# Norm roots and inverses on a fourth of the columns, and the first mixer's convolution dealt out anew

## What is computed

```python
def layer_norm(x, g, b):
    mu = jnp.mean(xf, axis=-1, keepdims=True)
    var = jnp.mean(jnp.square(xf - mu), axis=-1, keepdims=True)
    y = (xf - mu) * lax.rsqrt(var + EPS)
...
def conformer_conv(z, conv_w, conv_b, ln_g, ln_b):
    a, g = jnp.split(z, 2, axis=-1)
    h = a * jax.nn.sigmoid(g)
    h = causal_dwconv(h, conv_w, conv_b)      # 31 taps, 512 channels
    h = layer_norm(h, ln_g, ln_b)
    return jax.nn.silu(h)
...
# first layer ("even"): rms_norm, projection z, gelu on half of it,
#   layer norm "v", a spatial mixing, conformer_conv, output projection, FFN
# second layer ("odd"): attention, FFN; then rms_norm "final"
# second block, two layers: mixer, layer norm ln1, FFN, layer norm ln2
```

## Time and profile before

| | |
|---|---|
| median of 3 runs | 2508.51 us (2506.43 to 2509.03) |
| the profiled execution | 2508.29 us, its span 2506.6 us |
| TensorE matmuls busy | 96% of the span |
| VectorE, ScalarE, GpSimd busy | 56%, 43%, 5% |
| mean granted TensorE clock | 0.988 of full |

### The profile page before, as it was taken

One profiled execution on the slowest core, in us unless ns is written; L12 is line 12 of the kernel. 1 busy time (PEld: TensorE's weight loads), 2 busy tenths in 40 slices (PEclk: granted clock), 3 DMA queues, 4 the chain that ended last, 5 costly groups with the idle time before them and its releaser, 6 DMA issues.

```text
span 2506.6 us, 32833 instructions
## 1 busy us (share of the span) xinstructions
PE 2411.5 (96%) x11748; PEld 1912.8 (76%) x11748; DVE 1410.4 (56%) x2270; ACT 1083.7 (43%) x1673; POOL 125.7 (5%) x115
## 2 busy tenths in 40 slices
PE   8989999999999999999999989999989998999997
PEld 6657888887777888887777668888868766788885
DVE  5887777435765677732547764334353767533434
ACT  4444444326876444422447543233253663432322
POOL 0001000000000000001400010000113001000000
PEclk9999999999999999999999999999999999999999
DMA  4112222232121322222211122323222112232322
GB/s 174 61 42 93 99 94 99 94 101 68 59 67 59 101 92 100 92 101 96 103 60 35 51 72 96 100 94 101 93 100 74 43 35 76 76 101 93 101 93 76
DMA packets 57437, 210.61 MB, mean 84 GB/s; under 512 B 6478, under 2 KB 6880, under 8 KB 56960
## 3 DMA queue, kind: packets, MB, share of 16 engines
q1 hardware_dynamic: 56736, 204.51, 24.3%
q0 software_dynamic: 608, 4.81, 0.5%
HBM read 207.20 MB, written 2.10 MB: 83 GB/s over the span
## 4 chain that ended last, share of the span: by engine, by line
PE 67%; issue 22%; DVE 5%; POOLq 2%; ACT 2%; DVEq 1%; POOL 1%; DMA 0%; SPq 0%; ACTq 0%
PE PS L1150 12%; PE PS L1152 12%; PE PS L1151 12%; PE PS L1178 9%; PE PS L1180 9%; PE PS L1179 9%; PE PS L1209 1%; DVE CONV L1819 1%; DVE RSTD L1758 1%; POOLq L573 1%; PE PS L1264 1%; PE PS L1239 1%; PE PS L1242 1%; POOLq L582 1%; PE PS L1240 1%
## 5 line engine op out<-in xcount | busy, mean ns | idle before, releaser
L1744 DVE TENSOR_TENSOR WL<-RAW,WH 128x1024 fp32r<-128x1024 f32 x376 | 476.2, 1267 | 428.7 <-ACT WH L601 427.4
L1150 PE MATMUL PS<-HH,WH 128*128 128x512 f32 x1792 | 708.3, 395 | 7.0 <-DVE KR L1993 4.5
L1152 PE MATMUL PS<-HH,WL 128*128 128x512 f32 x1792 | 698.8, 390 | 0.0
L1151 PE MATMUL PS<-HL,WH 128*128 128x512 f32 x1792 | 698.6, 390 | 0.0
L601 ACT ACTIVATE WH<-RAW 128x1024 fp32r<-128x1024 f32 x376 | 397.1, 1056 | 696.4 <-PE PS L1180 411.0
L1150 PEld LDWEIGHTS PS<-HH,WH 128*128 128x128 f32 x1792 | 337.0, 188 | 84.4 <-issue 8.0
L1151 PEld LDWEIGHTS PS<-HL,WH 128*128 128x128 f32 x1792 | 337.2, 188 | 71.8 <-issue 3.6
L1152 PEld LDWEIGHTS PS<-HH,WL 128*128 128x128 f32 x1792 | 336.9, 188 | 70.8
L1180 PE MATMUL PS<-MH,WL 128*128 128x512 f32 x864 | 336.1, 389 | 0.0
L1178 PE MATMUL PS<-MH,WH 128*128 128x512 f32 x864 | 336.1, 389 | 0.0
L1179 PE MATMUL PS<-ML,WH 128*128 128x512 f32 x864 | 336.1, 389 | 0.0
(11 more groups left out here) (291 smaller groups left out, 2586.8 us busy)
## 6 DMA issues: line engine op xcount, KB each, us to landing
RAW<-wstream SPq DMA_DIRECT2D x376, 512.0 KB, 3.2
W<-cmp_w POOLq DMA_DIRECT2D x2, 2048.0 KB, 8.3
X<-xt SPq DMA_DIRECT2D x4, 512.0 KB, 6.5
out<-X SPq DMA_DIRECT2D x8, 256.0 KB, 2.0
TAB<-tables SPq DMA_DIRECT2D x1, 1871.5 KB, 13.1
WS<-spatial_w SPq DMA_DIRECT2D x1, 512.0 KB, 8.4
BS<-spatial_b SPq DMA_DIRECT2D x1, 256.0 KB, 9.0
PW<-pool_w POOLq DMA_DIRECT2D x2, 128.0 KB, 2.4
```

The costliest lines, as they stand in the source:

```text
L1150: pe.matmul(PS[:, bank, :], WH[:, b, w], HH[:, k, :], start=(k == 0), stop=False)
L1151: pe.matmul(PS[:, bank, :], WH[:, b, w], HL[:, k, :], start=False, stop=False)
L1152: last = pe.matmul(PS[:, bank, :], WL[:, b, w], HH[:, k, :], start=False, stop=(k == DC - 1))
L1744: dve.tensor_tensor(WL[:, b, :], RAW[:, b, :], WH[:, b, :].bitcast(F32), ALU.subtract).then_inc(w_lo, 1)
```

## The change

It has two halves.

First, six norms ("v", "final" and the four layer norms ln1 and ln2 of the second block) change how sum, root and inverse are laid out. `sum_quarters` multiplies the four quarters of the tokens (128 columns each) with ones of 128x32, and puts quarter q on partitions 32q to 32q+31 of 128 columns of one bank. The root and the reciprocal then cover 128x128 instead of 128x512. `widen` brings the result back: four matmuls, whose weights pick partition 32q, write the inverse of every token on all partitions of a PSUM bank. VectorE waits for that (`n_wide`) and scales its tiles with the PSUM bank instead of RSTD. The norms "even", "conv", "f0", "odd" and "f1" stay as they were.

Second, the convolution. TensorE keeps only 10 taps of chunk 3, in one group. VectorE adds the remaining 21 taps of chunk 3 (`last_chunk`), in a chain, and no longer has chunk 2. Chunks 0, 1 and 3 are accumulated in PSUM banks 4, 5 and 7; only the last tap writes to SBUF. For chunk 2 ScalarE writes 31 products (`products`), the first into CONV and 30 into a ring of five buffers, and GpSimd adds them one by one. The products are placed in ScalarE's order in groups of four (the last of three) beside the weight splits. The transposes of V now wait for chunks 0 and 1, because they use their banks, and VectorE waits for ScalarE's addition of the bias to bank 7 before step 14.

```diff
+DIAG = 10
+RING, RING_AT = 5, 3
+CONV_BANK = {0: 4, 1: 5, 3: 7}
 FF = 2816
 FC = FF // P
 FF2 = 4096
...
     t["identity"] = np.eye(P)
     t["ones"] = np.ones((P, P))
...
 
...
+        e_tap = sem("e_tap")
...
             pool.affine_select(out=WS[:], in_=WS[:], pattern=[[0, 2 * HC], [1, P]], base=0, channel_multiplier=-1,
                                compare_op=ALU.is_ge, fill=0.0).then_inc(e_mask, 1)
 
+            for k in range(1, TAPS):
...
+
 
             def fold(dst, src, last, ready, at):
 
@@ -614,7 +628,8 @@
                 n = NORM[nm][1]
...
             def rows_hi(buf, base):
                 for n in range(DC):
@@ -644,9 +659,24 @@
...
+            def products(first, last):
+
+                for k in range(first, last):
+                    src, w = CB[:, 2, k:k + T], vec("even_conv_w", 2 * TAPS + k)
+                    if k == 0:
+                        act.wait_ge(e_glu, 3)
+                        ins = act.activation(CONV[:, 2, :], src, ACT.Identity, scale=w, bias=vec("even_conv_b", 2))
+                    else:
+                        if k > RING:
+                            act.wait_ge(e_tap, k - RING)
+                        ins = act.activation(Y[:, RING_AT + k % RING, :], src, ACT.Copy, scale=w)
+                    ins.then_inc(e_prod, 1)
+
             for j in range(HC):
                 split_hi(0, 2 * j + 2)
                 split_hi(0, 2 * j + 3)
+                if j == HC - 1:
+                    products(0, 4)
                 act.wait_ge(e_z, 2 * j + 2)
                 if j:
...
                 gelu(s)
-                for k in range(*DIAG_PARTS[j:j + 2]):
-                    ins = act.activation(TAPD[:, k, :], tab("identity"), ACT.Identity,
-                                         scale=vec("even_conv_w", (HC - 1) * TAPS + k))
-                ins.then_inc(e_diag, 1)
+                if j == 0:
+                    for k in range(DIAG):
+                        ins = act.activation(TAPD[:, k, :], tab("identity"), ACT.Identity,
+                                             scale=vec("even_conv_w", (HC - 1) * TAPS + k))
+                    ins.then_inc(e_diag, 1)
+                products(4 + 4 * j, 8 + 4 * j)
             squares(NB, V, range(HC), n_cent, 0)
             split_hi(0, 14)
             gelu(12)
+            products(20, 24)
+            act.wait_ge(e_conv3, 1)
+            act.activation(PS[:, 7, :], PS[:, 7, :], ACT.Identity, bias=vec("even_conv_b", HC - 1)).then_inc(e_kept3, 1)
...
+            products(24, 28)
             split_hi(0, 16)
             gelu(14)
+            products(28, TAPS)
             for t in range(TT):
                 act.wait_ge(e_vt, t + 1)
                 act.activation(VTOK[:, t, :], PS[:, 2 + t, :], ACT.Copy).then_inc(e_vtok, 1)
             split_hi(0, 17)
-            act.wait_ge(e_conv3, 1)
-            act.activation(CONV[:, HC - 1, :], PS[:, 7, :], ACT.Identity, bias=vec("even_conv_b", HC - 1)).then_inc(e_kept3, 1)
...
+            def sum_quarters(src, bank, ready, first, final):
+
+                pe.wait_ge(*ready)
+                for q in range(TT):
+                    last = pe.matmul(PS[q * QUARTER:(q + 1) * QUARTER, bank, 0:P], tab("ones")[:, 0:QUARTER],
+                                     src[:, q * P:(q + 1) * P], start=first, stop=final)
+                if final:
+                    last.then_inc(n_sum, 1)
+
+            def widen(nm, bank):
+
+                pe.wait_ge(n_inv, WIDE[nm])
+                for q in range(TT):
+                    pick = tab("pick")[:, q:q + 1].to_broadcast([P, P])
+                    last = pe.matmul(PS[:, bank, q * P:(q + 1) * P], pick, STD[:, P:2 * P], start=True, stop=True)
+                last.then_inc(n_wide, 1)
...
+            def taps():
+
+                pe.wait_ge(e_glu, HC)
+                pe.wait_ge(e_diag, 1)
+                for k in range(DIAG):
+                    last = pe.matmul(PS[:, 7, :], TAPD[:, k, :], CB[:, HC - 1, k:k + T], start=(k == 0), stop=(k == DIAG - 1))
+                last.then_inc(e_conv3, 1)
...
-            taps(0)
+            taps()
             sum_rows(V, 2, [(n, e_gelu, n + 1) for n in range(HC)], n_add)
             tile(12)
             for n in range(HC):
-                sum_squares(NB, n, 3, "v", n == HC - 1)
+                sum_quarters(NB[:, n, :], 3, (n_sq, NORM["v"][0] + n + 1), n == 0, n == HC - 1)
+            widen("v", 6)
             tile(13)
-            taps(1)
             tile(14)
+            for n in range(2):
+                pe.wait_ge(e_conv[n], TAPS)
             for t in range(TT):
                 for n in range(HC):
                     pe.wait_ge(e_vaff, n + 1)
                     last = pe.transpose(PS[:, 2 + t, n * P:(n + 1) * P], V[:, n, t * P:(t + 1) * P], tab("identity"))
                 last.then_inc(e_vt, 1)
-            taps(2)
...
-            sum_rows(CONV, 6, [(0, e_conv, 2 * TAPS), (1, e_conv, 2 * TAPS), (3, e_kept3, 1), (2, e_conv, 3 * TAPS)], n_add)
+            sum_rows(CONV, 6, [(0, e_conv[0], TAPS), (1, e_conv[1], TAPS), (2, e_tap, TAPS - 1), (3, e_conv[3], TAPS - DIAG)], n_add)
...
-            sum_last(2, NBF[:, 0, :], NBF, n_sq, NORM["final"][0], "final", n_sum)
+            sum_quarters(NBF[:, 0, :], 2, (n_part, PART["final"]), True, False)
+            sum_quarters(NBF[:, DC - 1, :], 2, (n_sq, NORM["final"][0] + DC), False, True)
+            widen("final", 3)
 
             def layer_norm(nm):
                 sum_last(0, MU[:], X, x_ready, XR[nm], nm, n_add)
                 for n in range(DC):
-                    sum_squares(NB2, n, 3, nm, n == DC - 1)
+                    sum_quarters(NB2[:, n, :], 3, (n_sq, NORM[nm][0] + n + 1), n == 0, n == DC - 1)
+                widen(nm, 2)
...
+            def spread_wide(nm):
+
+                dve.wait_ge(n_std, NORM[nm][1] + 1)
+                dve.reciprocal(STD[:, P:2 * P], STD[:, 0:P]).then_inc(n_inv, 1)
+                dve.wait_ge(n_wide, WIDE[nm])
...
-                        dve.scalar_tensor_tensor(buf[:, n, :], src[:, n, :], vec(gain, n), RSTD[:], ALU.mult, ALU.mult)\
+                        dve.scalar_tensor_tensor(buf[:, n, :], src[:, n, :], vec(gain, n), PS[:, 3, :], ALU.mult, ALU.mult)\
                            .then_inc(n_row, 1)
...
-                src = CB[:, n, k:k + T]
+                src, acc = CB[:, n, k:k + T], PS[:, CONV_BANK[n], :]
                 w = vec("even_conv_w", n * TAPS + k)
                 if k == 0:
-                    ins = dve.tensor_scalar(CONV[:, n, :], src, w, vec("even_conv_b", n), ALU.mult, ALU.add)
+                    ins = dve.tensor_scalar(acc, src, w, vec("even_conv_b", n), ALU.mult, ALU.add)
                 else:
-                    dve.wait_ge(e_conv, before)
-                    ins = dve.scalar_tensor_tensor(CONV[:, n, :], src, w, CONV[:, n, :], ALU.mult, ALU.add)
-                ins.then_inc(e_conv, 1)
+                    if before:
+                        dve.wait_ge(e_conv[n], before)
+                    ins = dve.scalar_tensor_tensor(CONV[:, n, :] if k == TAPS - 1 else acc, src, w, acc, ALU.mult, ALU.add)
+                ins.then_inc(e_conv[n], 1)
...
-            def third_chunk(first, last):
+                        tap(n, k, k)
+
+            def last_chunk(first, last):
                 for k in range(first, last):
-                    tap(2, k, 2 * TAPS + k)
+                    tap(3, k, k - DIAG)
...
-            spread("v", RSTDV)
+            spread_wide("v")
             for n in range(HC):
-                dve.tensor_tensor(NB[:, n, :], V[:, n, :], RSTDV[:], ALU.mult).then_inc(n_row, 1)
+                dve.tensor_tensor(NB[:, n, :], V[:, n, :], PS[:, 6, :], ALU.mult).then_inc(n_row, 1)
             step(13)
             two_chunks(done + 9, TAPS)
+            dve.wait_ge(e_kept3, 1)
             step(14)
-            third_chunk(0, 22)
+            last_chunk(DIAG, 22)
             step(15)
-            third_chunk(22, TAPS)
+            last_chunk(22, TAPS)
...
-            spread("final")
...
-                spread(nm)
+                spread_wide(nm)
                 gain, bias = nm.replace("_", "_g"), nm.replace("_", "_b")
                 for n in range(DC + 1):
                     if n < DC:
-                        dve.scalar_tensor_tensor(NB2[:, n, :], X[:, n, :], vec(gain, n), RSTD[:], ALU.mult, ALU.mult)\
+                        dve.scalar_tensor_tensor(NB2[:, n, :], X[:, n, :], vec(gain, n), PS[:, 2, :], ALU.mult, ALU.mult)\
```

More of the change, by code:

```diff
@@ L110 @@
 VEC_EVEN = VEC_AT["odd_norm_g"]
-TABLES = [("identity", P), ("ones", P), ("eps", 2), ("swap2", P), ("cumulate", P), ("head_mean", P),
+TABLES = [("identity", P), ("ones", P), ("eps", 2), ("pick", TT), ("swap2", P), ("cumulate", P), ("head_mean", P),
           ("dilated", T), ("causal", T), ("cos", T), ("sin", T), ("cos2", T), ("sin2", T),
@@ L144 @@
     _at += _w
+WIDE = {n: i + 1 for i, n in enumerate(["v", "final"] + [f"ln{a}_{l}" for l in range(DEPTH2) for a in (1, 2)])}
+QUARTER = 32
```

(38 more changed lines are left out.)

2 lines of the change are left out of this document (removed).

## The result

The changed kernel took 2491.09 us (median of 6 runs, 2489.75 to 2492.73), the kernel before beside it 2507.11 (6 runs, 2506.37 to 2509.03): a ratio of 0.9935 with a 95% interval of 0.9925 to 0.9946, 16.0 us less. The forecast was 2490 in a range of 2480 to 2500. The profiled execution took 2491.1 with a span of 2489.3, 17.3 less than the span of before (2506.6).

A forecast was written before the change was run, and what follows sets the result against it. TensorE, busy 96% of the span, was taken as the bound, other engines counting only where it waits. Layer norms 14.4, norm final 1.3 and first mixer 2.7 sum to 18.4 us off 2508.3: forecast 2490, range 2480 to 2500.

The forecast's parts named there:

- A layer norm: Second block's four layer norms: quicker sums, root and reciprocal, less widening, save 3.6 us each, 14.4 in all.
- the widening: In each layer norm, spreading the inverse by TensorE adds 1.2 us; at half clock its records take 1.9 instead of 0.95.
- The norm final: At norm final only the shorter reciprocal, less the widening, counts: 1.3 us less, ends 0.5 and 2.
- The first mixer: VectorE's path through the first mixer: 17.8 us saved, 12.9 added, 2.2 for half clock, net 2.7 less.
- GpSimd's contention: In the first mixer, GpSimd's additions slow seven VectorE weight splits by 0.3 us each, 2.1 in all.
- rival (d): VectorE's taps and GpSimd's additions exclude one another: slower than before, 2517 us at 0.9 per addition; chance 0.06.
- The half clock at tile 13: TensorE idles some 7 us before tile 13 in the first mixer; half clock lasting 4.5 us then costs 2.2.
- PSUM as accumulator: VectorE's 83 convolution taps writing to PSUM cost the same as today; ends 5 us less and 10 more.
- Rival (b): PSUM accumulators cost 0.065 us more a tap, so the mixer loses 5.4 us: 2495 in all; chance 0.1.
- Rival (e): The mixer's end waits for GpSimd's last addition; at 2.2 us an addition it gives nothing: 2493; chance 0.07.
- Rival (c): The mixer gains 10 us, without half clock at tile 13 or GpSimd contention, with cheaper taps: 2482; chance 0.15.
- Rival (a): Quartered sums don't run side by side, so a layer norm gains only 1.5 us: 2498 in all; chance 0.12.

The follow-up runs named there:

- the quarters: Changed kernel plus idle quarter matmuls ahead of each layer norm's sums, sixteen on one column tile, then sixteen over four: 2490.74 us, one run.

## Why the prediction was right, step by step

- **A layer norm: right, 3.3 us on average for 3.6.** Sums 0.47 behind the last square (0.46 forecast), root 0.38 (0.39), reciprocal 0.96 (0.95). The term that was too good is the widening. I took the half clock to strike one norm in four; it struck all of them in the profiled execution to some degree: the widenings took 1.62, 2.07, 1.39 and 2.08 us in ln1_0, ln2_0, ln1_1 and ln2_1, against 1.16 at full clock. These lie about within the bounds (0.95 and 1.9, each without the passage of the last one), and 13.4 for 14.4 is their effect. Nor was this execution unlucky: in the seven profiled kernels whose layer norms are those of the change, 17 of 28 widenings took over 2.0 us and four took 1.16, and the four norms gave 12.5 to 14.1 us. The gain of a norm at half clock was forecast rightly (2.9, and 2.9 measured in ln2_1); how often the clock falls was not.
- **The norm final: right, 0.9 for 1.3.** The split of weights still stood ahead of the reciprocal, as in the earlier trace rows. From there to the first row it is 2.51 us, against 3.43; reciprocal's end to first row took 1.56 for 1.2.
- **The first mixer: 2.4 for 2.7 in this execution, 1.9 over four.** Waits at the gated unit (1.94 for 2.0), the split of tile 11 (2.76 for 2.7), the root (1.78 for 1.5), the widening, tile 13 and its split, with what the half clock adds to them (2.17 + 3.62 + 0.46 = 6.25 for 1.1 + 3.0 + 0.5 + 2.2 = 6.8). GpSimd's contention was put at 0.3 for each of seven splits, 2.1; it was 0.7 to 1.0 for three of them and 0.75 for the fourth gated unit, which I had not counted, 3.3 in all, of which 2.1 reach the end of the mixer. The row from which I took 0.3 was misread: its split starts at 1458.03, when an addition that ends at 1458.64 is running, so it was held for the last 0.6 us of one addition and no more. The two additions shown beside it begin only behind its end. Of the two operations with a PSUM operand in the same rows only the second overlaps an addition, and it starts first, so they said little on rival (d). In all, the costs were 16.0 us where the forecast had 15.1: the contention was dearer by 1.2, the group of tile 13 cheaper by 0.5, and it is luck that these partly cancel.
- **The half clock at tile 13: the row was read too simply.** I wrote that 5 us of idleness brought it, and costed 2.2. It came sooner: TensorE's last quartered sum of v ended at about 108.0, and the granted clock was 0.67 in 108 to 109, 0.50 in 109 to 118. In the three other executions of this mixer it came at 105.0, 105.1 and 106.8, while the sums of v were running or just begun, behind 2.2 us in which TensorE had nothing to do. Its cost lies in the widening (2.08 for 1.16) and in the beginning of tile 13, which started at 117.09 while the half clock lasted until 118.5: 0.9 + 0.7 = 1.6 us, an estimate. The size was about right, the cause given for it was not. With tile 13 ahead of the widening it came between 107 and 111 in four of five profiled executions and not in the fifth, and where the reciprocal came late anyway it cost nothing: the stretch was 125.55 with it and 125.63 without.
- **PSUM as accumulator: no price, as taken.** 0.66 and 0.79 us a tap, where SBUF had 0.667 and 0.786. The mean duration of a tap is 747 ns, but its successor starts before it ends. The 125 ns against 60 that the Trainium skill (Perfetto Trace Analysis, Optimizing Scalar/DVE Operations) gives didn't add anything to a row of such operations, writes included. Rival (b) falls.
- **Rival (e) falls:** GpSimd's last addition ended at 138.1, VectorE's last tap at 150.7. **Rival (c)** didn't come: contention and half clock were both there, and the taps were no cheaper. **Rival (a)** falls with the quarters, **rival (d)** with the accumulator in PSUM.
- **The sum:** 13.4 + 0.9 + 2.4 = 16.7 of the 17.3 between the spans; the medians of the runs are 16.0 apart. All three terms came out somewhat under the forecast 14.4 + 1.3 + 2.7 = 18.4. That the time is only 1.1 us above 2490 owes something to the kernel before, which ran 1.2 us faster beside the change than in the execution from which I counted (2507.1 against 2508.3).

## What to carry to other kernels

A reduction to a small result should be kept small until it is needed wide: root and reciprocal are paid by the column (2.7 us less), and widening by TensorE cost 1.2 to 2.1 of that, by the clock, provided that the pieces of the sum keep ahead of the engine that feeds them. When two engines are given elementwise work at once, look for the operation's tensors first: with one operand in PSUM VectorE's taps ran free beside GpSimd, with both in SBUF each tap beside an addition cost 1.0 us more and the whole gain was gone. And an operation that waits for another engine goes behind all the work in its queue that doesn't: one exchanged line was worth more than the whole convolution part.

## What the runs showed of the hardware

- VectorE beside GpSimd's additions: a tap with two SBUF tensors 1.7 us instead of 0.7, with its accumulator in PSUM 0.66; a split 1.9 to 2.2 instead of 1.22; a gated unit 1.50 instead of 0.75. The one that starts second waits: 0.86 us for a split that began with 1.00 of an addition left, 2.25 instead of 1.29 for an addition that began 0.13 behind a split. GpSimd's additions start 1.41 us apart when not disturbed and 1.70 beside taps in SBUF.
- The granted clock fell to 0.50 during or behind thin work (sums of 0.43 us in every 0.60) and short idleness (2.2 us ahead of the sums of v), also while TensorE was already at work again without a gap (busy 1.00 from 107 to 110 at 0.50). The level that came was 1.2 GHz each time. Idle work behind the sums put it 5 us later in ln1_0 and did not stop it in ln2_0; what starts it I could not settle.
- What it costs depends on where it falls: a widening takes 2.08 us instead of 1.16, ten records of idle matmuls 2.50 instead of 1.38, and nothing was lost behind the first row of a norm (355.6 us to the next squares with it and without).
- Quarter tiles: 0.22 us for a float32 matmul of 128 columns when the next uses the same tile, about 0.06 when four are used in turn.
